# A two-block transformer on one core: output products inside block 1's attention, the last layer norm applied token-major, and another order of the first transfers, splits and products

## The reference, cut to what matters

```
def layer_norm(x, g, b):
    xf = x.astype(jnp.float32)
    mu = jnp.mean(xf, axis=-1, keepdims=True)
    var = jnp.mean(jnp.square(xf - mu), axis=-1, keepdims=True)
    y = (xf - mu) * lax.rsqrt(var + LN_EPS) * g.astype(jnp.float32) + b.astype(jnp.float32)
    return y.astype(x.dtype)
...
    for l in range(DEPTH):          # block 1
        with_ctx = l < DEPTH - 1
        mod_x = (silu_c @ w_ada[l] + b_ada[l])[:, None, :]
        mod_c = (silu_cc @ w_ada[l] + b_ada[l])[None, None, :]
...
        hx = modulate(rms_norm(x, g_norm1[l]), sh1_x, sc1_x)
        hc = modulate(rms_norm(ctx, g_norm1[l]), sh1_c, sc1_c)
...
        x = x + gt1_x * (jnp.concatenate([oa, ob, oc], axis=-1) @ w_out[l])
...
    for l in range(DEPTH):          # block 2
...
        ff = squared_relu_mlp(x, w_ff1[l], w_ff2[l])
        x = layer_norm(ALPHA * x + ff, ln3_g[l], ln3_b[l])
    return x
```

## Time and profile before

| what | us |
|---|---|
| median of 3 runs | 3622.78 |
| lowest and highest | 3622.26, 3626.05 |
| the profiled execution's own time | 3624.62 |
| its span (first to last instruction) | 3622.8 |
| PE busy in it | 3502.8 |
| mean granted clock of TensorE | 0.986 |

### The profile page before, as it was taken

One profiled execution on the slowest core, in us unless ns is written; L12 is line 12 of the kernel. 1 busy time (PEld: TensorE's weight loads), 2 busy tenths in 40 slices (PEclk: granted clock), 3 DMA queues, 4 the chain that ended last, 5 costly groups with the idle time before them and its releaser, 6 DMA issues.

```text
span 3622.8 us, 49989 instructions
## 1 busy us (share of the span) xinstructions
PE 3502.8 (97%) x19778; PEld 2789.4 (77%) x19778; DVE 1650.7 (46%) x2977; ACT 1494.8 (41%) x2509; POOL 1455.7 (40%) x986
## 2 busy tenths in 40 slices
PE   7999889999999999999999999999999999999998
PEld 5776567888899776578888668878887668878886
DVE  5766645433343766643452685142113585142112
ACT  4445554433355436534333354433223354443222
POOL 4520013444488520025544444434444443434442
PEclk8999999999999999999999999999999999999999
DMA  7513512333365420523333212313333212313331
GB/s 232 157 54 106 181 37 86 99 99 96 97 185 163 132 58 14 175 76 101 99 99 102 71 53 82 105 55 103 99 96 87 71 53 78 110 53 105 96 97 64
DMA packets 640912, 355.57 MB, mean 98 GB/s; under 512 B 68917, under 2 KB 613289, under 8 KB 640681
## 3 DMA queue, kind: packets, MB, share of 16 engines
q1 hardware_dynamic: 628827, 339.66, 32.2%
q10 hardware_dynamic: 11854, 12.72, 1.1%
HBM read 346.28 MB, written 6.05 MB: 97 GB/s over the span
## 4 chain that ended last, share of the span: by engine, by line
PE 89%; DVE 5%; ACT 3%; issue 2%; DMA 1%; POOL 1%; SPq 0%; ACTq 0%; DVEq 0%
PE psum L882 67%; PE psum L1114 5%; PE psum L1145 3%; PE psum L1165 2%; PE psum L906 1%; DVE neg_max L2006 1%; PE psum L1086 1%; ACT work L1573 1%; PE psum L990 1%; PE psum L910 1%; PE psum L1194 1%; PE psum L1046 1%; DMA w_ada_first<-in_w_ada_dram 1%; PE psum L1172 1%; PE psum L1025 1%
## 5 line engine op out<-in xcount | busy, mean ns | idle before, releaser
L865 POOL TENSOR_TENSOR w_lo<-w_raw,w_hi 128x256 fp32r<-128x256 f32 (+3 forms) x936 | 1393.7, 1509 | 2103.5 <-ACT w_hi L1416 2103.2
L882 PE MATMUL psum<-h_hi,w_hi 128*128 128x512 f32 (+1 forms) x2736 | 1035.3, 378 | 2.5 <-POOL w_lo L865 1.5
L882 PE MATMUL psum<-h_hi,w_lo 128*128 128x512 f32 (+1 forms) x2736 | 1010.6, 369 | 0.0
L882 PE MATMUL psum<-h_lo,w_hi 128*128 128x512 f32 (+1 forms) x2736 | 1010.0, 369 | 0.0
L1416 ACT ACTIVATE w_hi<-w_raw 128x1024 fp32r<-128x1024 f32 (+1 forms) x546 | 571.2, 1047 | 676.9 <-PE psum L882 655.1
L882 PEld LDWEIGHTS psum<-h_hi,w_hi 128*128 128x128 f32 x2736 | 516.4, 189 | 110.4 <-issue 18.7
L882 PEld LDWEIGHTS psum<-h_lo,w_hi 128*128 128x128 f32 x2736 | 516.5, 189 | 93.0 <-issue 8.9
L882 PEld LDWEIGHTS psum<-h_hi,w_lo 128*128 128x128 f32 x2736 | 516.0, 189 | 87.9
L882 PE MATMUL psum<-hid_hi,w_hi 128*128 128x512 f32 (+1 forms) x1040 | 388.2, 373 | 1.8 <-POOL w_lo L865 1.8
L882 PE MATMUL psum<-hid_hi,w_lo 128*128 128x512 f32 (+1 forms) x1040 | 386.9, 372 | 0.0
L882 PE MATMUL psum<-hid_lo,w_hi 128*128 128x512 f32 (+1 forms) x1040 | 386.7, 372 | 0.0
(11 more groups left out here) (238 smaller groups left out, 4114.7 us busy)
## 6 DMA issues: line engine op xcount, KB each, us to landing
w_raw<-in_w_up_dram SPq DMA_DIRECT2D x132, 512.0 KB, 3.7
w_raw<-in_w_ff_dram SPq DMA_DIRECT2D x128, 512.0 KB, 3.7
w_raw<-in_w_in_dram SPq DMA_DIRECT2D x92, 512.0 KB, 3.7
w_raw<-in_w_ada_dram SPq DMA_DIRECT2D x80, 512.0 KB, 4.1
w_raw<-in_w_down_dram SPq DMA_DIRECT2D x48, 512.0 KB, 3.4
w_raw<-in_w_mkv_dram SPq DMA_DIRECT2D x32, 512.0 KB, 3.7
w_raw<-in_w_down_dram SPq DMA_DIRECT2D x24, 384.0 KB, 3.0
w_ada_first<-in_w_ada_dram SPq DMA_DIRECT2D x4, 2048.0 KB, 18.2
```

What stands on the lines that cost most here:

```text
L865: m = nc.gpsimd.tensor_tensor(WL[:, c % NSPLIT, k:k + step, :], RAW[:, c % NRAW, k:k + step, :], WH[:, c % NSPLIT, k:k + step, :].bitcast( ...
L882: m = pe.matmul(out_ap, lhs(a, k), rhs(b, k), start=(k == 0 and n == 0), stop=(k == nk - 1 and n == 2))
```

## The change

Three places are changed.

1. **The start.** SP issues all four `w_ada` pieces, then the tiles, with the lambdas behind tile 2. The 12 parameter rows go to ACT's queue, behind the gain rows. PE turns block 0's rows at once, and has dummy products (`keep_busy`) between. ACT takes each `first_row` as soon as it can, and splits tiles 0 and 1 before the last four squares of `ctx` and the last `first_row`.
2. **Block 1's attention.** Twelve units of the output product of `x` (slices 0 to 5 of its first two tiles, in banks 7 and 3, in layer 1 banks 7 and 1) stand in the four rounds behind the last step of the attention of `x`, in both layers. In layer 0 the other 52 are spread over the `ctx` attention anew, and in rounds that transpose a mixed step the units stand before the transposes. ACT splits the third tile of `w_out` in the last but one step.
3. **The end.** ACT copies each turned slice token-major into `out_nat` beside the products. Behind the statistics ACT applies 1/std and -mean/std per token (a per-partition scale and bias), DVE multiplies with the gain row, and the bias row is added on POOL for the even and on DVE for the odd of 8 pieces of 128x512. SP stores each piece, 256 KB.

```diff
-            for i in range(4):
-                if i == 3:
-                    sp.wait_ge(*at("turned", "first_rows"))
-                    rest_of_rows()
...
+                if c == NRAW:
+                    lambdas()
...
-        UNITS = [range(13 * i // 5, 13 * (i + 1) // 5) if i < 20 else range(52 + 3 * (i - 20), 55 + 3 * (i - 20)) for i in range(24)]
+        TAIL_UNITS = {(0, "turn"): [(0, i) for i in range(4)], (1, "value"): [(0, 4), (0, 5), (1, 0)],
+                      (2, "spread"): [(1, 1), (1, 2)], (3, "end"): [(1, 3), (1, 4), (1, 5)]}
+        LATE_UNITS = [(n, i) for n in range(2) for i in (6, 7)]
+        STEP_UNITS, left = [], LATE_UNITS + [(n, i) for n in range(2, KT) for i in range(KT)]
+        for n in [2] * 12 + [3, 2, 2, 2, 3, 2, 2, 2] + [3, 3, 2, 2]:
+            STEP_UNITS.append(left[:n])
...
+                    tail(i, "turn")
+                    mixed = turned is not None and steps[i - 1]["mix"] is not None
+                    if beside is not None and mixed:
+                        beside(i)
                     if turned is not None:
                         turn(turned["fills"][:2])
-                    if beside is not None:
+                    if beside is not None and not mixed:
                         beside(i)
...
+            first_turn(0)
             first_block(1)
-            first_turn(0)
-            rms_stat(("n1", "x", 0))
+            pe.wait_ge(*at("turned_taken", ("in", 11)))
+            keep_busy(2, 3)
             first_block(2)
             first_turn(1)
-            rms_stat(("n1", "c", 0))
+            keep_busy(1, 3)
+            rms_stat(("n1", "x", 0))
+            keep_busy(1, 3)
             first_block(3)
             first_turn(2)
+            rms_stat(("n1", "c", 0))
             first_turn(3)
...
+                    if att["one_out"] and i == len(steps) - 4 + AHEAD:
+                        split_beside_norm(IDS["out", S[1], S[2]][0])
...
+            def slice_out(n):
+
+                act.wait_ge(*at("ln_stat", (LAST, n, 3)))
+                nc.scalar.activation(OUTS[:, :, n * P:(n + 1) * P], PS[:, ln_stat_bank(LAST, n), :].rearrange("p (t c) -> p t c", c=P),
+                                     ACT.Copy).then_inc(*mark("slice_copied", n))
...
+            for u in range(8):
+                t = u // 2
+                nc.scalar.activation(out_piece(u), out_piece(u), ACT.Identity, bias=LN_SHIFT[:, t:t + 1],
+                                     scale=LN_STD[:, t:t + 1]).then_inc(*mark("out_normed", u))
...
+            for u in range(8):
+                dve.wait_ge(*at("out_normed", u))
+                nc.vector.tensor_tensor(out_piece(u), out_piece(u), row_piece(0, u), ALU.mult).then_inc(*mark("out_gained", u))
+                if u not in ADD_ON_POOL:
+                    dve.wait_ge(*at("out_gained", u))
+                    nc.vector.tensor_tensor(out_piece(u), out_piece(u), row_piece(1, u), ALU.add).then_inc(
+                        *mark("out_ready", u))
...
+            for u in ADD_ON_POOL:
+                pool.wait_ge(*at("out_gained", u))
+                nc.gpsimd.tensor_tensor(out_piece(u), out_piece(u), row_piece(1, u), ALU.add).then_inc(*mark("out_ready_pool", u))
```

More of the change, by code:

```diff
@@ L479, in _, with lambdas @@
         def _(sp):
-            def rest_of_rows():
-                pieces = [piece for name in PCOL if name not in FIRST_ROWS + ("gains",) for piece in row_pieces(name)]
-                for n, (a, to, view) in enumerate(pieces):
-                    sp.dma_start(to, view).then_inc(*mark("rows_in", "last" if n == len(pieces) - 1 else a, 16))
+            def lambdas():
                 for i, name in enumerate(("lambda_q1", "lambda_k1", "lambda_q2", "lambda_k2")):
@@ L1060, in out_ready, with out_unit, out_proj @@
                 return ready
-            def out_proj(S, cs, T, att, ln=None, other=None):
+            def out_unit(S, cs, ready, n, k):
+                if k == 0:
+                    pe.wait_ge(*at("w_lo", cs[n]))
+                if n == 0:
+                    pe.wait_ge(*ready(k))
+                for m, (a, b) in enumerate(((WH, HH), (WH, HL), (WL, HH))):
+                    ins = pe.matmul(PS[:, unit_bank(S, n), :], a[:, cs[n] % NSPLIT, k, :], b[:, k, :], start=(k == 0 and m == 0),
+                                    stop=(k == KT - 1 and m == 2))
+                if k == KT - 1:
+                    ins.then_inc(*mark("w_used", cs[n]))
+            def out_proj(S, cs, T, att, ln=None, other=None, begun=False):
                 for n in range(KT):
@@ L1065, in out_proj @@
                         pe.wait_ge(*at("resid", (S, n - 4)))
+                    if begun and n < 2:
+                        for i in (6, 7):
+                            out_unit(S, cs, out_ready(att), n, i)
+                        continue
                     if other is not None and n == 2:
@@ L1098, in attend, with tail @@
                     pe.wait_ge(*signal)
+                def tail(i, place):
+                    if S[:2] == ("att", "x"):
+                        out = ("out", "x", S[2])
+                        for n, k in TAIL_UNITS.get((i - len(steps), place), ()):
+                            out_unit(out, IDS[out], out_ready(att), n, k)
                 def bank_free(b):
@@ L1158, in attend @@
                         before = o - 1 if att["one_out"] else o - 2
+                        if u["first"] and o == 1:
+                            for signal in before_odd:
+                                pe.wait_ge(*signal)
                         if u["first"] and before >= 0:
@@ L1175, in attend @@
                         m.then_inc(*mark("pv_done", (S, q)))
+                    tail(i, "value")
                     ada(S, i, ada_rows)
@@ L1212, in attend @@
                         m.then_inc(*mark("sub_spread", (S, o)))
+                    tail(i, "end")
             def ffn(S, cs, T, groups, parts, normed, ln=None, before_last=None):
@@ L1427, in gain_rows, with rest_of_rows @@
                             *mark("gains_in", "last" if (l, i) == (DEPTH - 1, len(GAINS) - 1) else (name, l), 16))
+            def rest_of_rows():
+                pieces = [piece for name in PCOL if name not in FIRST_ROWS + ("gains",) for piece in row_pieces(name)]
+                for n, (a, to, view) in enumerate(pieces):
+                    act.dma_start(to, view).then_inc(*mark("rows_in", "last" if n == len(pieces) - 1 else a, 16))
             split_early = set()
@@ L1646, in ffn @@
                             beside_residual(S, step[1] * KT, step[2], T, x, rms, ln, first)
+                            if ln == LAST and step[2]:
+                                slice_out(step[2] - 1)
                         continue
```

129 lines of the change are left out of this document (75 added, 54 removed).

## The result

| | before | after |
|---|---|---|
| median | 3624.1 us (4 runs, 3622.26 to 3626.05) | 3604.7 us (4 runs, 3604.26 to 3609.1) |
| ratio | | 0.9949, 95% interval 0.9932 to 0.9966 |
| the profiled execution | 3624.6 us, span 3622.8 | 3604.3 us, span 3602.5 |
| mean granted clock | 0.986 | 0.989 |

The account below looks back on a forecast made before the run. PE, busy 97% of the span, was taken as the bound, with gains only where it idles, runs slowly or has finished. Terms 8.8 + 5.5 + 8.2 + 4.6 = 27.1 off 3624.6, less 1.8, gave 3595.7 us, range 3584 to 3606.

Parts of the forecast that it names:

- rival of the other sign: ctx attention: thinner rounds with waits keep TensorE at 1.2 GHz throughout, 3656 us in all; chance 0.02.
- its queue did not stall: Start: rival had ACT's row transfers stall, first copy at 34 not 25, gain 3 not 8.8, 3601.5 us; chance 0.10.
- the four terms: Gains of start 8.8, layer 1 tail 5.5, layer 0 tail 8.2 and end 4.6 us, each with bounds.
- tile 1 lands near 38: Start: with the fourth w_ada piece landing near 34.3, weight tile 1 follows near 38 us, tile 2 near 40.
- the sum and PE's `rms_stat` end at 41.9: Start: after ACT's last first_row at 41.1, sum and rms_stat end at 41.9, so the norm starts at 44.1 us.
- if the norm still starts at 49: Start: stated sign of being wrong; the norm was expected near 44 us, from 49.51 before.
- Behind which all keeps its distance: Start: everything after the first two tiles keeps the 8.8 us gained by having them near 52.9, not 61.7.
- 12 x 0.69 - 1.6 = 6.7: Layer 0, tail of the attention of x: 12 units done at 0.69 us each, tail ending 1.6 later, net 6.7 us.
- The 1.5 for the clock: Layer 0: faster slow first units of the ctx attention give 1.5 us, making 8.2 with the tail's 6.7.
- The reordering, priced at 0 with -2 to +5: Layer 0, mixed ctx rounds: units before transposes trade 6.3 us of mix waits for 6.6 elsewhere; costed at nothing.
- 13.4 us: End: DVE's 12 passes (8.2 us) and POOL's 4 (5.2) take turns, so 13.4 us in series, to 3615.1.
- the sharing itself would cost 2.5: End: with no passes on POOL, 16 DVE passes would take 10.9 us, so sharing with POOL costs 2.5.

Follow-up runs that it names:

- run with the sums alone: Changed kernel, but POOL begins w_lo of tile 1 only when DVE has added the last squares of ctx: 3606.2 us in one run.
- run with the squares first: Changed kernel, but ACT does the last four squares of ctx and the fourth row's copy before splitting the first weight tiles: 3602.59 us.

## Why the prediction was right, and where its sizes were off

**The bound and the sign** held. All of the 20 us lie where PE idled or ran slowly, or behind its last product, and no rival of the other sign showed. The fourth `w_ada` piece (36.66), ACT's first row (24.82, so its queue did not stall), the waits behind the transposes and the turns of DVE and POOL are all as described. That the time lies in the range, by 1 us, is in part luck: two of the changed kernel's eight runs are above 3606, and the start and layer 0 fell short by 10.6 us, of which the end and the clock between the layers gave 3.8 back. The bounds of the four terms were also added wrongly: they make 3583 and 3604, not 3585 and 3603.

**The start: 8.8 forecast, 3.7 measured.** Two steps failed, and by them the norm started at 49.79 and not at 44.1, 5.7 us late. The first is "tile 1 lands near 38". It was at ACT at 40.94, and the squares behind it began 2.8 us late. Most of that was there with the fourth `w_ada` piece, which PE waited for until 36.66 and which was to land at 34.3; why, no run tells. The second is "the sum and PE's `rms_stat` end at 41.9". The sums were priced as free, though I had POOL's `w_lo` running "by 43.3" a few lines further, and the earlier trace rows open before me. I used that row for the end and not for the start. From the first of the four squares to the end of `rms_stat` it took 5.0 us (41.90 to 46.89) instead of 2.8 (39.1 to 41.9), and 1.5 of these 2.2 are the turns with POOL, by the run with the sums alone. The other 0.7 came behind `rms_stat`. The run with the squares first showed one more thing that the sum left out: with the norm at 42.3, PE waited 5.03 us for `w_lo`, so an earlier norm alone wins little. The forecast had named its own sign of failure here, "if the norm still starts at 49", and it does. "Behind which all keeps its distance" was right for what follows the first two tiles.

**Layer 0: 8.2 forecast, 2.7 measured.** The step that failed is the net formula "12 x 0.69 - 1.6 = 6.7". Twelve units are 8.3 us of PE's time, and PE idled 4.6 us there. They cannot lie in that and lengthen the tail by only 1.6: it must grow by 3.7 at least, and the gain is at most the 4.6. Measured, PE's idle time from 230 to 480 us fell by 3.6 (20.26 to 16.62), and the tail's end came 2.8 us later than before (474.74 to 477.50), though the first copy had been 3.7 earlier. So the way there grew by 6.5 us. That is, nearly, 8.3 for the units, less the 3.6 of idle time, plus 1.7 more lost to the clock before that point. The 1.5 for the clock did not come: both executions lost 8.5 from 230 to 480 us. In the rounds idle time grew from 7.8 to 9.9 and the clock gave 1.7 back. The reordering, priced at 0 with -2 to +5, cost 1.6 (90.7 to 89.1). The waits that I listed for it were near (1.8, 1.1, 1.8 and 1.9 against 1.60, 1.01, 1.60 and 1.99), but the list was not complete: 1.35 for the mix in the third mixed round and 0.65 for the second spread stayed.

**Layer 1: 5.5 forecast, 5.2 measured.** The same net formula stood here with 9 units. It holds better since PE's idle time and the slow products behind it could take them: from 1548 to 1562 the changed kernel is busy for 13.49 of 14 us at full clock:

```profile
1548.00:1562.00 14.00, 13.49 (x111) 11.13 (x108) 5.04 (x11) 4.76 (x11) 0.10 (x1) 1.00 0.01 2
```

In the forecast, the clock's part was 0.9; the two cannot be told apart in one execution. And that 5.2 came so near to 5.5 is luck: the second execution of the same kernel lost 6.8 us less to the clock in this stretch, and by it the gain is 9.3. What the runs show is that the tail is filled; the gain over the kernel before, of which there is one execution, is 3.4 to 9.4 in the ten executions with this attention of layer 1.

**The end: 4.6 forecast, 6.9 measured.** DVE and POOL take turns, as said. "13.4 us" was mis-sized: 16 passes end to end at their recorded durations, and the chain of twelve and four took 11.6. DVE's share of it was near (0.684 a pass summed up, 1.33 for two in the kernel without POOL's part, so 8.0 for twelve). What was too dear is POOL's pass: 1.30 in the sum, 0.9 in the chain, which is (11.6 - 8.0)/4. The rest is the last store: 2.5 us from the end of DVE's last pass (3599.98) to the end of the span, against 3.1 assumed. Against the forecast's own claim that "the sharing itself would cost 2.5", it cost 1.0.

**Layer 0 to layer 1: 0 forecast, 1.5 measured.** No edit is there. It is the clock: the four executions that lost 1.7 us in this stretch, the kernel before and the second one of the changed kernel among them, take 608.2 to 608.5 us for it, and the eight that lost nothing take 606.2 to 607.0.

## What to carry to other kernels

- Work put into a wait wins at most the wait. Write the idle time of the stretch beside the length of what goes in, and let the difference lengthen the stretch, before any other term.
- When two engines have been seen to take turns in one place of a trace, look for every other place of the new order where the same two meet. Here the change moved a split ahead by 6 us and with it POOL's work beside DVE's sums.
- Units that fill a round can stand on both sides of the step in the middle: one ahead where its input is late, the others behind where its result is late. All ahead was the worst here (9.9 us idle). All behind had no more idle time than the division (8.0 each), but longer single waits and 3.4 us more of the lower clock; that the waits were the cause is not shown.
- Take a second profiled execution before a gain of a few us is put down to an edit. Here the same kernel differed by 4.1 us in one stretch.

## What the runs showed of the hardware

- **DVE and POOL.** A DVE sum of two SBUF inputs (128x256) took 0.42 us alone and 0.84 beside POOL's `w_lo` of 128x256 (3.36 for four, 2.72 for six alone). At the end the sum of 128x512 took 1.64 with a POOL sum of 1.68 over it, 0.69 alone. The Trainium skill (SBUF — State Buffer, "Who interferes with whom") has one of the two block the other for a whole instruction; these rows agree, and by the kernel with the sums alone it is 1.5 us at the start. In the norm the cost falls on the other engine: with the squares first, DVE's passes mostly stayed at 0.48 us and POOL's pieces took 0.84 us each beside them (10.03 for twelve), against 0.69 each in four that ran with DVE idle but for the last 0.2 us, in the kernel with the sums alone:

```profile
39.55 2.77 POOL L892 TENSOR_TENSOR w_lo<-w_raw,w_hi 128x256 fp32r<-128x256 f32 x4 [39.13 <-ACT w_hi L1475]
```

- **The clock of TensorE.** An unchanged kernel lost 27.3 us and 22.2 us to the lower level in two executions (60 to 3580 us), 8.5 and 10.3 in the same 250 us of layer 0, and 11.95 and 5.1 in layer 1. Kernels whose attention was the same lost 8.5 to 13.65 in those 250 us. So one trace cannot price an edit's effect on the clock of the whole below some 5 us. Yet in the `ctx` rounds the loss was the same within 0.05 us in seven executions (5.1), and changed with the order alone (6.8, 5.1, 3.4).
